# K/V scratch stores of a diffusion layer: seven DMAs on ScalarE's queue become three on SyncE's

## What is computed

```python
xc = ffn_sublayer(xc, mod, 0, ...)                       # x + 0.5*gate*swiglu(modulate(rmsnorm(x)))
h = modulate(xc, norm_mix[l], mod[..., 3, :], mod[..., 4, :])
dq, dk, dv, gq, gk, gv = mixer_projections(h, w_in[l], q_norm[l], k_norm[l])
...
# latent tokens: the same with rotary positions, and keys/values of the cache ahead of their own
dk_all = jnp.concatenate([cache_diff_k[:, l], dk], axis=1)
dv_all = jnp.concatenate([cache_diff_v[:, l], dv], axis=1)
o_diff = sweep_query_blocks(lambda q, k=dk_all, v=dv_all: diff_attn_block(q, k, v, lam), (dq,))
o_gqa = sweep_query_blocks(lambda q, k=gk_all, v=gv_all: gqa_block(q, k, v), (gq...,))
xs = xs + mod[..., 5, :][..., None, :] * mixer_output(o_diff, o_gqa, ...)
xs = ffn_sublayer(xs, mod, 2, ...)
```

## Time and profile before

| | |
|---|---|
| median of 2 timed runs | 6739.27 us (6735.11 to 6743.42) |
| the profiled execution's own time | 6517.78 us |
| its span on the slowest core, core 2 | 6516.2 us |
| spans of the 8 cores | 6438.3 to 6516.2 us |
| PE busy | 4311.4 us, 66% of the span |
| DVE busy | 2922.7 us, 45% |
| ACT busy | 1900.6 us, 29% |
| POOL busy | 1507.4 us, 23% |
| moved by DMA | 565.48 MB, mean 87 GB/s |
| granted PE clock, mean | 0.805 on core 2 |

### The profile page before, as it was taken

How to read it: one execution, slowest core, us unless ns; L and a number is a source line. 1 busy time by engine, 2 the same in 40 slices (tenths; PEclk the granted TensorE clock), 3 DMA queues, 4 the chain that set the end, 5 groups by cost and what they waited for, 6 DMA issues and landing times.

```text
span 6516.2 us, 62014 instructions; the slowest of 8 cores (6438.3 to 6516.2 us)
## 1 busy us (share of the span) xinstructions
PE 4311.4 (66%) x17311; PEld 1796.2 (28%) x17311; DVE 2922.7 (45%) x3356; ACT 1900.6 (29%) x2344; POOL 1507.4 (23%) x1267
## 2 busy tenths in 40 slices
PE   3483378748558656875773667846677566856678
PEld 1131133323224333432332222312223122322223
DVE  0011342243222222223223888257872788448882
ACT  0011111121111111111112656136551555325551
POOL 1001000000000000000000667036650557216660
PEclk7776567758779878887886889978888888978888
DMA  9789313212422333333241111221113002121113
GB/s 153 172 189 131 62 63 115 84 36 81 152 96 97 117 111 106 118 111 111 97 146 64 37 37 56 96 68 37 37 63 127 30 30 69 64 76 42 36 51 105
DMA packets 316120, 565.48 MB, mean 87 GB/s; under 512 B 55362, under 2 KB 254474, under 8 KB 287114
## 3 DMA queue, kind: packets, MB, share of 16 engines
q1 hardware_dynamic: 218106, 480.83, 22.9%
q0 software_dynamic: 53616, 41.42, 6.0%
q10 hardware_dynamic: 44064, 39.27, 1.9%
HBM read 563.61 MB, written 80.68 MB: 99 GB/s over the span
## 4 chain that ended last, share of the span: by engine, by line
PE 40%; POOL 21%; DVE 15%; DMA 7%; issue 6%; ACT 6%; ACTq 2%; another core or an unknown queue 1%; POOLq 1%; DVEq 0%; SPq 0%
PE PSA L277 38%; POOL ACCS L653 20%; DVE ON L673 5%; DMA XN<-w_ada 3%; ACTq L411 2%; ACT XN L427 2%; PE PSA L432 2%; DVE RT L443 1%; DVE HT L435 1%; DMA s_gu<-w_ff_gu 1%; POOL SM L416 1%; ACT JUNK L423 1%; ACT ARENA L644 1%; DVE RT L510 1%
## 5 line engine op out<-in xcount | busy, mean ns | idle before, releaser
L653 POOL TENSOR_TENSOR ACCS<-ACCS,ARENA 128x256 f32<-128x256 f32 (+1 forms) x1152 | 1376.0, 1194 | 995.7 <-ACT ARENA L644 431.7
L651 DVE TENSOR_TENSOR ACCS<-ACCS,ARENA 128x768 f32<-128x768 f32 (+1 forms) x1152 | 1386.1, 1203 | 135.6 <-ACT ARENA L644 21.3
L644 ACT ACTIVATE ARENA<-PSA 128x1024 bf16<-128x1024 f32 (+1 forms) x1216 | 1191.2, 1002 | 553.4 <-POOL ACCS L653 259.2
L277 PE MATMUL PSA<-HT,AR 128*128 128x512 bf16 x5632 | 1267.6, 390 | 4.1 <-DVE HT L435 4.1
L416 POOL TENSOR_TENSOR SM<-SS,NEGH 128x4 f32<-128x4 f32 (+2 forms) x52 | 85.3, 1640 | 3814.8 <-DVE SS L414 3814.8
L277 PE MATMUL PSA<-ARENA 128*128 128x512 bf16 x2304 | 711.4, 391 | 296.3 <-ACT ARENA L644 295.2
L277 PE MATMUL PSA<-QT,ARENA 128*128 128x512 bf16 x2304 | 730.7, 404 | 68.8 <-DVE ON L673 53.6
L277 PEld LDWEIGHTS PSA<-HT,AR 128*128 128x128 bf16 x5632 | 561.5, 100 | 707.3 <-issue 164.9
L277 PE MATMUL PSA<-BR,ARENA 128*128 128x512 bf16 x2816 | 682.1, 403 | 61.6 <-DVE RT L443 54.2
L467 DVE TENSOR_TENSOR ARENA<-SG,PSA 128x512 bf16<-128x512 f32 x352 | 242.1, 688 | 1028.1 <-PE PSA L277 1007.5
L432 PE MATMUL PSA<-IDF,XN 128*128 128x128 f32 x960 | 240.3, 403 | 583.4 <-ACT XN L427 559.7
(11 more groups left out here) (91 smaller groups left out, 2069.0 us busy)
## 6 DMA issues: line engine op xcount, KB each, us to landing
AR<-s_gu SPq DMA_DIRECT2D x176, 1024.0 KB, 5.8
BR<-s_dn SPq DMA_DIRECT2D x352, 256.0 KB, 2.8
XN<-w_ada SPq DMA_DIRECT2D x36, 1024.0 KB, 6.3
ARENA<-s_kt SPq DMA_DIRECT2D x64, 576.0 KB, 3.8
AR<-s_in SPq DMA_DIRECT2D x32, 1024.0 KB, 8.5
s_gu<-w_ff_gu POOLq DMA_DIRECT2D x44, 512.0 KB, 43.9
ARENA<-s_vd SPq DMA_DIRECT2D x32, 576.0 KB, 3.7
ARENA<-s_vg SPq DMA_DIRECT2D x32, 576.0 KB, 3.7
```

The source lines that it names most:

```text
L277: return e.matmul(out, lhsT, rhs, start=start, stop=stop, **kw)
L644: P.op("act", (lambda e: e.activation(PT2[:, slot, :, 0:nq], PSA[:, 2 * r:2 * r + 2, 0:nq], AF.Exp, scale=0.125)), reads=[PK(2 * r), PK(2 ...
L651: P.op("dve", (lambda e: e.tensor_tensor(out=ACCS[:, :, 0:cs], in0=ACCS[:, :, 0:cs], in1=PT2[:, slot, :, 0:cs], op=ALU.add)), reads=[("PT" ...
L653: P.op("pool", (lambda e: e.tensor_tensor(out=ACCS[:, :, cs:nq], in0=ACCS[:, :, cs:nq], in1=PT2[:, slot, :, cs:nq], op=ALU.add)), reads=[( ...
```

## The change

Three things are done to the stores.

1. `VD` and `VG` are laid out head first, then subtile. The copies that write them and the attention code of the prompt that reads them index accordingly; sizes stay.
2. `store_kv` issues three stores and not seven: `KT` as before, all four heads of `VD` in one, both heads of `VG` in one. In each partition a head's four subtiles are now one run of 512 elements (1 KB) on both sides.
3. `store` gets a parameter `q`. The three stores of `store_kv` and the store of X to `s_x1` are issued on SP. All other stores stay on ACT.

```diff
-    VD = sb("VD", [128, NT, 4, 128], BF16)
-    VG = sb("VG", [128, NT, 2, 128], BF16)
+    VD = sb("VD", [128, 4, NT, 128], BF16)
+    VG = sb("VG", [128, 2, NT, 128], BF16)
...
-    def store(out_ap, in_ap, rkeys, wkeys=()):
+    def store(out_ap, in_ap, rkeys, wkeys=(), q=None):
...
-        P.op(STQ[0], lambda e: e.dma_start(out=out_ap, in_=in_ap), reads=list(rkeys), writes=list(wkeys), dma=name)
+        P.op(q or STQ[0], lambda e: e.dma_start(out=out_ap, in_=in_ap), reads=list(rkeys), writes=list(wkeys), dma=name)
...
-                P.op("dve", (lambda e, t=t: e.tensor_copy(VD[:, t, :, :], PSB[4 + t].rearrange("p (h d) -> p h d", d=128))),
+                P.op("dve", (lambda e, t=t: e.tensor_copy(VD[:, :, t, :], PSB[4 + t].rearrange("p (h d) -> p h d", d=128))),
...
     def store_kv(kt0):
-        store(s_kt[:, :, kt0 * 128:kt0 * 128 + ST].rearrange("c p n -> p c n"), KT[:, :, :], [("KT", c) for c in range(5)], [("s_kt", kt0)])
-        for h in range(4):
-            store(s_vd[h, :, kt0:kt0 + NT, :], VD[:, :, h, :], ["VD"], [("s_vd", h, kt0)])
-        for n in range(2):
-            store(s_vg[n, :, kt0:kt0 + NT, :], VG[:, :, n, :], ["VG"], [("s_vg", n, kt0)])
+        store(s_kt[:, :, kt0 * 128:kt0 * 128 + ST].rearrange("c p n -> p c n"), KT[:, :, :], [("KT", c) for c in range(5)], [("s_kt", kt0)], q="sp")
+        store(s_vd[:, :, kt0:kt0 + NT, :].rearrange("h p t e -> p h (t e)"), VD[:, :, :, :].rearrange("p h t e -> p h (t e)"),
+              ["VD"], [("s_vd", h, kt0) for h in range(4)], q="sp")
+        store(s_vg[:, :, kt0:kt0 + NT, :].rearrange("n p t e -> p n (t e)"), VG[:, :, :, :].rearrange("p n t e -> p n (t e)"),
+              ["VG"], [("s_vg", n, kt0) for n in range(2)], q="sp")
...
                 store(s_x1[(idx - 4) * ST:(idx - 3) * ST, :].rearrange("(t p) f -> p t f", p=128), Xc[:, :, :],
-                      [("X", xcur[0], t) for t in range(NT)], [("s_x1", idx - 4)])
+                      [("X", xcur[0], t) for t in range(NT)], [("s_x1", idx - 4)], q="sp")
```

More of the change, by code:

```diff
@@ L584, in mix_kv @@
                 P.op("act", (lambda e, t=t: e.activation(R1[:, t, :], PSB[4 + t], AF.Copy)), reads=[PK(4 + t)], writes=R1K)
-                P.op("dve", (lambda e, t=t: e.tensor_copy(VD[:, t, :, :], R1[:, t, :].rearrange("p (h d) -> p h d", d=128))),
+                P.op("dve", (lambda e, t=t: e.tensor_copy(VD[:, :, t, :], R1[:, t, :].rearrange("p (h d) -> p h d", d=128))),
                      reads=R1K, writes=["VD"])
             else:
-                P.op("dve", (lambda e, t=t: e.tensor_copy(VD[:, t, :, :], PSB[4 + t].rearrange("p (h d) -> p h d", d=128))),
+                P.op("dve", (lambda e, t=t: e.tensor_copy(VD[:, :, t, :], PSB[4 + t].rearrange("p (h d) -> p h d", d=128))),
                      reads=[PK(4 + t)], writes=["VD"])
@@ L602, in mix_kv @@
                 P.op("act", (lambda e, t=t: e.activation(QB[:, t, 0:128], R0[:, t, 0:128], AF.Copy)), reads=R0K, writes=["QB"])
-            P.op("dve", (lambda e, t=t: e.tensor_copy(VG[:, t, :, :].rearrange("p n (r d) -> p n r d", r=2),
+            P.op("dve", (lambda e, t=t: e.tensor_copy(VG[:, :, t, :].rearrange("p n (r d) -> p n r d", r=2),
                                                       R0[:, t, 128:256].rearrange("p (h d) -> p h d", d=64).unsqueeze(2).broadcast_to([128, 2, 2, 64]))),
@@ L702, in attn_prompt @@
                     kts.append(((lambda t=t, h=h: KT[:, h, t * 128:(t + 1) * 128]), [("KT", h)],
-                                VD[:, t, h, :], ["VD"]))
+                                VD[:, h, t, :], ["VD"]))
                 attn_unit("diff", h, (0, 1), bb * 256, 256, kts)
@@ L709, in attn_prompt @@
                         kts.append(((lambda t=t: KT[:, 4, t * 128:(t + 1) * 128]), [("KT", 4)],
-                                    VG[:, t, n, :], ["VG"]))
+                                    VG[:, n, t, :], ["VG"]))
                     attn_unit("gqa", n, (2 * gp, 2 * gp + 1), bb * 256, 256, kts)
```

## The result

The changed kernel takes 0.9707 of the time of the kernel before, 95% interval 0.9672 to 0.9742. The medians over all executions are 6377.48 us (6280.47 to 6623.52, 11 runs) after and 6628.87 us (6465.58 to 6761.23, 10 runs) before. In some executions of both kernels a part of the cores gets a lower PE clock and the time is up to 5% longer; the ratio compares the others.

What follows compares the result with a forecast made beforehand. ACT's store issues, delaying the next norm's squares and so PE at nine boundaries, were taken as the bound. On core 3, 146.4 + 16.5 - 9 = 154 us; profiled 157 us less, so 6739 - 157 = 6582 us, range 6350 to 6640.

Steps and rivals of the forecast that it cites:

- The sign: Whole kernel: faster, chance 0.73; within 2% had 0.24 and slower 0.03.
- How that stands to the median: Whole kernel: the profile's 157 us gain subtracted unchanged from the two timed runs' 6739 us, giving 6582.
- the choice of the core: Launch end: core 3, 2.6 us behind core 2 with a smaller stall, becomes the core that counts; 154 us gained.
- part 1: Nine tile boundaries: the wait of the norm's first squares behind ACT's stores disappears, 146.4 us on core 3.
- Squares at T + 0.1: Tile boundaries, ACT: the next norm's squares start 0.1 us after the last KT copy ends (T), 0.9 us over nine.
- SP past its stores at T + 1.5: Tile boundaries, SP: the three K and V stores are issued by 1.5 us after the last KT copy ends (T).
- First AR block 0 to 38 us late, taken as 9: Nine boundaries: loads queued behind SP's stores delay the next stage's first AR block, 0 to 38 us in all, 9 charged.
- Store of X: 16.5 us: Four tiles: with X's store off ACT, scaling follows the residual 4.12 us sooner each, 16.5 us in all.
- Layout: nothing: VD and VG copies: the new layout costs 0 us, or 3 us if each VD copy took 0.1 us more.
- Rival 1: Tile boundaries: SP's issues are as slow as ACT's or loads come late; 81 us gained, 6658 us; chance 0.14.
- Rival 2: FFNs: PE's clock falls to 0.81, costing 20 us each; eight take the whole gain; chance 0.06.

Runs made afterwards that it cites:

- the third trace: Kernel before, unchanged, profiled once more; core clocks were 0.812 to 0.820 and spans 6437.7 to 6475.3 us.
- the loads-first run: Changed kernel with store_kv held back on SP until the next FFN's first four AR loads are issued; ratio to before 0.9707.
- the run with one wait more: Kernel before, with SP's next-tile loads waiting until the V stores have landed; the faster two of four executions took 6338.39 and 6347.06 us.
- the earlier trace: First profile of the kernel before, unchanged, on which the prediction was based; its profiled execution took 6517.8 us.

## Why the prediction was wrong

The mechanism was right in its main part: the stall left ACT, and the path from T to the matmul became shorter by nearly all of it. The sign was right; the number, 6582 us, was not. That the median, 6377 us, lies inside the range given is luck: it depends on how many of the eleven executions had a lower clock, and the five without one took 6280 to 6295 us, below the range's low end of 6350. Two steps failed.

**The level to which the gain was applied.** The step "How that stands to the median" took the two timed runs, 6739 us, as the kernel's time and subtracted from it. Their clocks are not on record, but all others of before with such a time had a lower clock on at least four cores. Over ten runs the median of before is 6628.87 us, and executions without such a clock take 6456 to about 6520 us, while those of the changed kernel take 6280 to about 6310. Against 6629 a forecast of 6582 is a gain of 47 us, and the medians moved by 251. The prediction saw the other level, named the 0.81 clock, counted eleven FFNs that would explain the 221 us, and still kept the higher level, without evidence that the changed kernel would be measured in it. The profiled execution's own 6518 us was the better base, but not free of it either: cores 2 and 3, its slowest, ran their first three FFNs at 0.81 and came to the first boundary at 1694 and 1708 us, the other six at 1629 to 1649. 157 us less is 6361, still 50 to 80 us above the 6280 to 6310. From 6466 us, the fastest of the ten runs of before, the same 157 would have given 6309.

**The size, through the choice of the core.** The gain in the ratio is 2.9%, 190 us of 6500 (168 to 213 by the interval), where 157 was forecast (2.4%). The term that was too small is part 1. I took the smallest stall of the eight, core 3's 147.3 us, because that core was nearly the slowest in that one trace; it was so because of the clock of its first FFNs. But the stall is not a property of a core: the third trace has 147 to 179 us, with 147.0 on core 4 and 164.1 on core 3. After the change the spread of the stall is gone for all of them. From T to matmul the eight cores lost 36.5 and 36.8 us a boundary and now lose 19.0: 158 to 160 us in nine. The mean stall, 162 to 165 us, was the better term: it is 15 to 18 us more than core 3's.

The other steps, by their own numbers:
- *Squares at T + 0.1.* They start 0.1 us before the trace's end of the copy, all nine times. Right.
- *SP past its stores at T + 1.5.* Measured T + 2.3; the V stores need 0.41 and 1.06 us, the second more than its fewer pieces would suggest. X goes out at T + 8.0 (range given 5.4 to 9.9).
- *First AR block 0 to 38 us late, taken as 9.* Measured 0.4 to 14.1 us in all on a core. The mechanism is real, shown by the loads-first run; the mean of the cores is 4.9 us, so the charge was too high by 4 us.
- *Store of X: 16.5 us.* Measured 17 to 18 us; the scaling comes 3.01 us after the residual, as forecast, and the `s_in` blocks were late by 0.3 us once.
- *Layout: nothing.* The copies cost nothing that shows in s1, and packets fell exactly as counted. But that merging and layout by themselves remove most of the stall (T + 21.1 and T + 23.5 on ACT) was not said in part 1, which put the gain down to the route. The stall of "12 to 23 us" was core 2's; over all cores it is 5 to 25.
- *Rival 1* (issue as slow on SP). It did not come, but its reason was good: the run with one wait more and the loads-first run show that it is competing loads that make an issue slow. SP was quick because its stores now stand ahead of its own loads. The Trainium skill, "DMA: Bandwidth & Descriptors", section "Issuing engines are not separate DMA queues", says that issuing from several engines saves only the issue time and that all share the same engines; the runs agree on the sharing, since loads on SP slow the issues on ACT (4.5 us without them, 11.5 to 22.6 us at the boundaries of the earlier trace rows), and they show that the issue time, which the page calls usually small, was what this sharing made large.
- *Rival 2* (the clock takes it back). It did not come: the mean granted clock of the changed kernel's cores 0 to 3 is 0.829 to 0.830, not lower than the 0.805 to 0.821 of before, and the gate and up half of no s1 FFN took more than 79 us on any core. The Trainium skill, "TensorE: Matmul & The Clock Gate", knows a level of 13/16 as a limit on the peak current of a whole die. The 0.81 of the earlier trace rows agrees with that level. That it takes a whole die is not what the trace of before shows: from 1110 to 1130 us of each core's span, in the same FFN, the clock is 0.81 on cores 2 and 3 and 1.00 on cores 0 and 1.

**The sum, again.** Between the third trace of before and the changed kernel s1 is 190 us shorter on the mean of the cores: 160 at the boundaries, 17 to 18 from the store of X, and 12 to 13 that remain. In that trace six of the eight cores had one s1 FFN whose gate and up half took 92 to 93 us in place of 76, which is 12 us of the mean. With the first trace of before, whose s1 had none of these, it is 174 us, 158 + 17 and nothing left. So the change itself is worth 174 to 178 us in s1. In the terms of the prediction's sum: 163 + 17 - 5 = 175 us on the mean of the cores, in place of 146.4 + 16.5 - 9 = 154 on core 3.

**What stays open.** Phase s2 was 2853 and 2855 us on the mean of the cores in the two traces of before and 2844 to 2851 in the changed kernel and its variants, most at 2844 to 2847 (the merge on ACT with the store of X on SP is left out for its clock). It is also 2846 in the kernel before with one wait more, whose s2 is the old code, so neither layout nor queue is needed for it; why s2 is some 8 us shorter after a shorter s1 was not found.

## What to carry to other kernels

When a compute engine also issues stores, look at how long its issues last and who stands behind them: here seven instructions that move 1.4 MB held ACT, and through it PE, for 5 to 25 us, 18 on the mean, at each of nine places. There are three cures, and each alone gave most of the gain: longer contiguous pieces, another queue whose later work can wait, or just not letting a burst of loads go out at the same moment. The three do not add up, since they remove the same stall. And a timed median of two runs is no base for a forecast: forecast the ratio, and take the mean over the cores for a cost that varies among them.

## What was not expected of the hardware

- The length of a DMA issue depends on what the DMA engines have to do, and not only on the instruction. The same store of VG (256 pieces of 1 KB) took 1.06 us ahead of the loads and 7.86 us behind 6 MB of them; seven stores of 3712 pieces took 4.5 us on ACT with no load beside them and up to 24 us with loads.
- Both small pieces and loads beside them are needed for a long stall on ACT's own queue: with pieces of 1 KB, 1408 in all, seven issues beside the same loads cost 5 us.
- A wait added to the loads made the kernel faster by some 125 us (best executions 6338 against 6465 us).
